# Reciprocal root in seven dependent steps instead of nine, and half of the residual addition on VectorE, in a two-layer transformer trunk

## The reference

```python
def rmsnorm(x, g):
    y = xf * lax.rsqrt(jnp.mean(xf * xf, axis=-1, keepdims=True) + NORM_EPS)
    return (y * g).astype(x.dtype)
...
for i in range(DEPTH):
    a = rmsnorm(h, norm_mix_pre[i])
    m = nsa_mixer(a, ...) if i % 2 == 0 else dilated_mixer(a, ...)
    h = h + rmsnorm(m, norm_mix_post[i])
    f = swiglu(rmsnorm(h, norm_ffn_pre[i]), ffn_w_gu[i], ffn_w_down[i])
    h = h + rmsnorm(f, norm_ffn_post[i])
return h
```

## Time and profile before

| | us |
|---|---|
| median of 3 runs | 898.27 (898.04 to 899.47) |
| the profiled execution, its own time | 895.89 |
| its span, first to last instruction | 894.2 |
| PE busy in it | 848.3 (95%) |
| DVE busy | 535.8 (60%) |
| ACT busy | 476.8 (53%) |
| POOL busy | 60.0 (7%) |
| mean granted TensorE clock | 0.991 of full speed |

### The profile page before, as it was taken

One profiled execution on the slowest core, in us unless ns is written; L12 is line 12 of the kernel. 1 busy time (PEld: TensorE's weight loads), 2 busy tenths in 40 slices (PEclk: granted clock), 3 DMA queues, 4 the chain that ended last, 5 costly groups with the idle time before them and its releaser, 6 DMA issues. The chain is left out here.

```text
span 894.2 us, 12740 instructions
## 1 busy us (share of the span) xinstructions
PE 848.3 (95%) x4345; PEld 688.7 (77%) x4345; DVE 535.8 (60%) x1119; ACT 476.8 (53%) x819; POOL 60.0 (7%) x134
## 2 busy tenths in 40 slices
PE   6999999999999999989999789999789999999995
PEld 5898666778888888768887578888568788888874
DVE  5888777586655555586544445545466865555533
ACT  7786666664544444465554554555565654444431
POOL 3000038020000000110000000000001100000002
PEclk9999999999999999999999899999999999999998
DMA  7666100454755556437556015555204367655611
GB/s 253 209 197 230 48 2 1 133 174 144 234 187 190 186 185 193 139 118 236 188 188 182 6 48 161 176 180 188 95 2 155 122 217 218 205 165 186 212 47 48
DMA packets 90107, 135.20 MB, mean 151 GB/s; under 512 B 6304, under 2 KB 55504, under 8 KB 90064
## 3 DMA queue, kind: packets, MB, share of 16 engines
q1 hardware_dynamic: 89392, 132.53, 46.2%
q0 software_dynamic: 576, 2.10, 0.7%
q10 hardware_dynamic: 96, 0.02, 0.0%
HBM read 133.59 MB, written 1.05 MB: 151 GB/s over the span
## 5 line engine op out<-in xcount | busy, mean ns | idle before, releaser
L954 DVE TENSOR_TENSOR w_lo<-w_raw,w_hi 128x1024 fp32r<-128x1024 f32 x248 | 301.3, 1246 | 110.1 <-ACT w_hi L528 106.0
L1385 PE MATMUL ps<-w_hi,xt_hi 128*128 128x512 f32 x784 | 314.6, 401 | 2.2 <-DVE xt_lo L984 1.7
L1385 PE MATMUL ps<-w_hi,xt_lo 128*128 128x512 f32 x784 | 307.3, 392 | 0.0
L1385 PE MATMUL ps<-w_lo,xt_hi 128*128 128x512 f32 x784 | 306.9, 391 | 0.0
L528 ACT ACTIVATE w_hi<-w_raw 128x1024 fp32r<-128x1024 f32 x248 | 252.8, 1056 | 40.8 <-DMA w_raw<-in_ffn_w_gu 20.2
L1385 PEld LDWEIGHTS ps<-w_hi,xt_hi 128*128 128x128 f32 x784 | 148.5, 189 | 32.4 <-DVE xt_lo L984 2.5
L1385 PEld LDWEIGHTS ps<-w_hi,xt_lo 128*128 128x128 f32 x784 | 148.4, 189 | 31.4
L1385 PEld LDWEIGHTS ps<-w_lo,xt_hi 128*128 128x128 f32 x784 | 148.8, 190 | 28.3
L780 ACT ACTIVATE st_hi<-ps 128x256 fp32r<-128x256 f32 x44 | 16.9, 384 | 113.4 <-PE ps L1394 113.4
L1385 PE MATMUL ps<-w_hi,st_hi 128*128 128x512 f32 x176 | 69.1, 392 | 3.0 <-DVE st_lo L1246 2.8
L506 POOL TENSOR_TENSOR h<-h,tmp 128x512 f32<-128x512 f32 x16 | 24.2, 1529 | 707.8 <-DVE tmp L1222 707.8
(11 more groups left out here) (176 smaller groups left out, 779.3 us busy)
## 6 DMA issues: line engine op xcount, KB each, us to landing
w_raw<-in_ffn_w_gu SPq DMA_DIRECT2D x88, 512.0 KB, 4.7
w_raw<-in_dil_w_in SPq DMA_DIRECT2D x72, 512.0 KB, 4.0
w_raw<-in_ffn_w_down SPq DMA_DIRECT2D x44, 512.0 KB, 4.1
w_raw<-in_nsa_w_in SPq DMA_DIRECT2D x20, 512.0 KB, 4.6
w_raw<-in_nsa_w_o SPq DMA_DIRECT2D x8, 512.0 KB, 4.6
w_raw<-in_dil_w_o SPq DMA_DIRECT2D x8, 512.0 KB, 4.0
w_raw<-in_nsa_cmp_wk SPq DMA_DIRECT2D x4, 512.0 KB, 5.0
w_raw<-in_nsa_cmp_wv SPq DMA_DIRECT2D x4, 512.0 KB, 3.9
```

The lines of the kernel that those rows point to most:

```text
L954: dve.tensor_tensor(w_lo[:, n.slot, c:c + 1024], w_raw[:, n.raw, c:c + 1024], w_hi[:, n.slot, c:c + 1024].bitcast(F32), ALU.subtract)\
L1385: ins = pe.matmul(o, s, m, start=start, stop=stop)
```

## The change

The root gets a first guess in one integer-free operation (the bits of `v` read as a number, multiplied and added), one Newton-like step with tuned constants and one third-order step. `add_post` adds the second half of the columns on DVE; POOL adds the first half only. `h_ready` becomes two semaphores, one for each half, and POOL's load of the next gain waits for DVE's addition too.

```diff
-        nt = sb("nt", [P, 4])
+        nt = sb("nt", [P, 6])
-        h_ready = [sem(f"h_ready{b}") for b in range(5)]
+        h_ready = [[sem(f"h_ready{b}_{half}") for half in range(2)] for b in range(5)]
...
             for b in range(1, 5):
-                for q in range(2 * MT):
-                    m, c = q // 2, slice(512 * (q % 2), 512 * (q % 2) + 512)
-                    pool.wait_ge(post_ready[b], q + 1)
-                    pool.tensor_tensor(h[:, m, c], h[:, m, c], tmp[:, m, c], ALU.add).then_inc(h_ready[b], 1)
+                for m in range(MT):
+                    pool.wait_ge(post_ready[b], m + 1)
+                    pool.tensor_tensor(h[:, m, 0:512], h[:, m, 0:512], tmp[:, m, 0:512], ALU.add)\
+                        .then_inc(h_ready[b][0], 1)
                 if b < 4:
+                    pool.wait_ge(h_ready[b][1], MT)
                     post_gain(b + 1, *nexts[b])
...
             def rsqrt(total, dst):
-                v, hv, y, t = (nt[:, i:i + 1] for i in range(4))
-                dve.tensor_scalar(hv, total, -0.5 / D, -0.5 * EPS, ALU.mult, ALU.add)
-                link(dve.tensor_scalar(v, total, 1.0 / D, EPS, ALU.mult, ALU.add))
-                link(dve.tensor_scalar(y.bitcast(I32), v.bitcast(I32), 1, None, ALU.logical_shift_right))
-                link(dve.tensor_scalar(y.bitcast(I32), y.bitcast(I32), -1.0, float(0x5F3759DF),
-                                       ALU.mult, ALU.add))
-                for i in range(3):
-                    link(dve.scalar_tensor_tensor(t, y, hv, y, ALU.mult, ALU.mult))
-                    last = dve.scalar_tensor_tensor(y if i < 2 else dst, t, 1.5, y, ALU.add, ALU.mult)
-                    if i < 2:
-                        link(last)
-                return last
+                v, hv, hk, y, t, y15 = (nt[:, i:i + 1] for i in range(6))
+                link(dve.tensor_scalar(v, total, 1.0 / D, EPS, ALU.mult, ALU.add))
+                dve.tensor_scalar(hv, total, -0.5 / D, -0.5 * EPS, ALU.mult, ALU.add)
+                link(dve.tensor_scalar(y.bitcast(I32), v.bitcast(I32), -0.5, RS_MAGIC, ALU.mult, ALU.add))
+                link(dve.scalar_tensor_tensor(t, y, hv, y, ALU.mult, ALU.mult))
+                dve.tensor_scalar(hk, hv, RS_K * RS_K, None, ALU.mult)
+                link(dve.scalar_tensor_tensor(y, t, RS_A, y, ALU.add, ALU.mult))
+                dve.tensor_scalar(y15, y, 1.5 * RS_K, None, ALU.mult)
+                link(dve.scalar_tensor_tensor(t, y, hk, y, ALU.mult, ALU.mult))
+                link(dve.scalar_tensor_tensor(t, t, 5.0 / 3.0, t, ALU.add, ALU.mult))
+                return dve.scalar_tensor_tensor(dst, t, 1.25, y15, ALU.add, ALU.mult)
...
                 for half in range(2):
                     c = slice(512 * half, 512 * half + 512)
-                    dve.scalar_tensor_tensor(tmp[:, m, c], bank(2 * m + half), rs_post[:, m:m + 1],
-                                             g_post[:, c], ALU.mult, ALU.mult).then_inc(post_ready[b], 1)
+                    ins = dve.scalar_tensor_tensor(tmp[:, m, c], bank(2 * m + half), rs_post[:, m:m + 1],
+                                                   g_post[:, c], ALU.mult, ALU.mult)
+                    if half == 0:
+                        ins.then_inc(post_ready[b], 1)
+                link(ins)
+                dve.tensor_tensor(h[:, m, 512:D], h[:, m, 512:D], tmp[:, m, 512:D], ALU.add)\
+                   .then_inc(h_ready[b][1], 1)
```

More of the change, by code:

```diff
@@ L64 @@
 INF = 3.0e38
+RS_MAGIC, RS_A, RS_K = float(0x5F210000), 1.207094421068867, 1.3861413103946667
 N_CMPKV, N_SEL, N_WIN, N_WK1, N_WV1, N_Q, N_NSAO = 0, 2, 4, 6, 8, 10, 14
@@ L427, in _ @@
                 m, half = q // 2, q % 2
-                sp.wait_ge(h_ready[4], q + 1)
+                sp.wait_ge(h_ready[4][half], m + 1)
                 sp.dma_start(out[0, m * P:(m + 1) * P, half * 512:(half + 1) * 512],
@@ L1661, in turn_m0 @@
                     for half in range(2):
-                        pe.wait_ge(h_ready[b], half + 1)
+                        pe.wait_ge(h_ready[b][half], 1)
                         xt_turn(b, 0, half, h)
@@ L1667, in turn_h2 @@
             def turn_h2(m, half):
-                pe.wait_ge(h_ready[2], 2 * m + half + 1)
+                pe.wait_ge(h_ready[2][half], m + 1)
                 xt_turn(2, m, half, h)
@@ L1710, in turn_h @@
                     for half in range(2):
-                        pe.wait_ge(h_ready[b], 3 + half)
+                        pe.wait_ge(h_ready[b][half], 2)
                         pe.wait_ge(xt_ready[b], 1 + half)
```

## The result

The changed kernel takes 892.93 us (median of 6 runs, 891.49 to 893.41) against 897.96 us of the kernel before (6 runs, 896.86 to 899.47): ratio 0.9942, 95% interval 0.9929 to 0.9955. That is faster by 5.0 us where 3.8 was forecast; 892.93 lies just inside the stated range, at its lower edge, the forecast time of 894.4 is missed by 1.5, and the forecast ratio 0.9957 lies just outside the interval of this comparison. The profiled execution took 893.11 us with a span of 891.4, which is only 2.8 us less than the profiled execution before. Three numbers for one change, 5.0, 3.8 and 2.8, are what the experiments had to sort out.

What follows compares the result with a forecast made beforehand. PE bounds the kernel (busy 95%), so only its waits behind changed lines count: 0.60 + 0.75 + 1.10 + 0.63 + 0.75 = 3.83 us, giving 892.06 profiled, plus 2.38 to the median: 894.4 us (ratio 0.9957), range 892.9 to 896.5.

Steps and rivals of the forecast that it cites:

- The rival that it saves nothing: All roots on DVE: ten instructions for ten save no time, so the change gains only 2.03 us (896.2); chance 0.07.
- The addition and POOL: In add_post, T being its first product's start: DVE's addition, ready at T + 1.43, waits for POOL until T + 1.97.
- Rival 3: DVE's addition isn't shut out by POOL: seam 2 gains 0.5 us more, time 893.9; chance 0.10.
- The five places: Where PE waits behind changed lines: the start, three seams between parts of the kernel, and the end; 3.83 us together.
- seam 1: Between block 1 and the first feed-forward part: PE gets xt_lo earlier, gain 0.75 us, bounds 0.4 and 0.95.
- seam 3: After the attention: PE gets xt_lo earlier, the third split waiting for a load; gain 0.63 us, bounds 0.3 and 0.7.
- the end: After the last matmul: h complete 0.95 us earlier, second store queues 0.2; gain 0.75, bounds 0.4 and 1.0.
- the start: First block: PE waits for gw_lo behind two roots on DVE; gain 0.60 us, range 0.2 to 0.6.
- The cover of the first split: At the seams: the first split starts 0.3 us later but costs nothing; without cover 0.3 at each of three seams.
- Seam 2, "DVE is late next": Before the attention: gain 1.10 us; PE no longer waits for h, about 1.2 of idle time stays at the rotation.
- Rival 1: Gains partly absorbed by slack at hid_r and loads at seam 1 and seam 3: 2.1 us, 896.2; chance 0.13.
- Rival 4: Slower: gaps at seam 2 or in the attention drop the granted clock for longer; four stretches make 901.2; chance 0.05.

## What held of the prediction, and the step that failed

- **The root**: 1.67 forecast, 1.64 measured. The rival that it saves nothing (the Trainium skill, VectorE: DVE Perf Modes, section "The DRAIN you can't avoid") fell: ten instructions for ten, two links fewer, 0.33 saved.
- **The addition and POOL**: forecast from T + 1.97 to T + 2.66; measured end T + 2.65 (886.14 to 888.79). The rule of the Trainium skill (SBUF — State Buffer, section "Who interferes with whom") holds here, shown by the kernel with the product in PSUM: 0.69 in place of 1.24 beside the same addition of POOL. Rival 3, that the two overlap, fell. What this made of the change: POOL's half saves DVE nothing, shown by the kernel without POOL.
- **The five places**: forecast 3.83, measured 3.74 and 3.82 in two profiles, and 3.9 over twelve runs at equal clock (4.5 as they stand). That the sums agree so closely is in part luck, since single terms were off both ways: seam 1 0.55 and 0.68 for 0.75, seam 3 0.86 and 0.49 for 0.63 (the arrival of a load in front of the third split shifts from one execution to the next), the end 0.84 and 0.85 for 0.75, the start 0.36 in one profile. There PE ran 1.33 late, 0.60 by the first loads and 0.73 at the lower clock, so that `gw_lo` no longer held it and the last 0.3 of the term couldn't be won.
- **The cover of the first split** was wrong in a small way: "for a piece that PE uses only after the current one". At seam 2 PE uses it at once and waits 0.17 for it (0.57 with the old root). It cost nothing only because PE waits for the rotation behind it anyway.
- **Seam 2, "DVE is late next"**: right, 1.11 left at the rotation plus the 0.17; taking the rotation forward removed the wait and gave 1.18 for the expected 1.0.
- **Rival 1** happened in part: in the first block PE lost 0.54, 0.2 and 0.2 of the start's gain in three of the variants, and nothing in the two profiles of the changed kernel. **Rival 4** had a real mechanism, but too small to turn the result: against the kernel before, the attention took from 1.5 us less to 2.8 us more over eight profiles, 0.8 and 2.1 more in those of the changed kernel. None of this is tied to the size of the gains at the seams.
- **The step that failed** is the last of the sum: "The median of the runs stands 2.38 higher, at 898.27, and gives 894.4." It took the distance between one profiled execution and the median of three as fixed, and the granted clock as the same on both sides. In the changed kernel the median stood 0.18 below its profiled execution (892.93 and 893.11) and in its second measurement 0.87 below (893.03 and 893.90). The profiled execution of the kernel before was a fast one, at a clock of 0.991 where its 35 later runs have 0.9877, and its median of three a slow one: the 35 runs have 897.38, 0.9 less than 898.27. That is 0.9 of the 1.5 us by which 894.4 was missed. The remaining 0.6 is what the fit gives to the changed kernel's higher clock, and its cause stays open as said above. The runs of a kernel scatter by 1.3 us, mostly with the clock, so a median of six against six can be off by about 1 us: the first comparison said 5.0, the second, with the same kernel, 0.9959, which is 3.7.

## What to carry to other kernels

Match the instructions of the bound engine in both traces one by one before believing a difference of spans: here the places that the change touches gave 3.7 and 3.8 us in two profiles, while an untouched stretch moved by up to 4 us between profiles, with the granted clock. Take the level of a forecast from many runs: a median of three was 0.9 us off here, a quarter of the change. When work is shared between DVE and POOL, count the SBUF inputs: two of them on DVE beside a POOL instruction that reads SBUF make the second engine wait, and moving one input to PSUM undid that. A queue is late at its next instruction too, so after removing a wait look at what else stands in front of the same engine's next product; the order of two splits and a rotation was worth a quarter of the whole change again.

## What the runs showed of the hardware that was not expected

In every profile taken the granted clock falls to its lower level near the start of both attention halves, for 3.4 to 10.2 us in all at each. The mean clock over the same 30 us was between 0.83 and 0.94 in kernels that are alike there. Against the kernel before, PE lost 0.1 to 0.8 us where it was 0.83 in place of 0.89 and 1.7 to 2.3 us where it was 0.83 in place of 0.94. No change of this study controls it. With every root doubled the clock also fell behind idle times of PE of 4.03 and 2.55 us at places where it otherwise stays up. DVE's root steps are so short that a filler instruction nobody waits for costs 0.07 us and a linked one 0.18 to 0.25: what such a chain of one-column operations costs is mostly its links: ten instructions with two links fewer took 0.33 less.
